# Modulation pieces summed on VectorE and recurrent gates in tiles of whole blocks, in a two-block transformer kernel

## What is computed

```python
mod = (c_act @ w_ada[l] + b_ada[l])[:, None, :]
shift1, scale1, gate1, shift2, scale2, gate2 = jnp.split(mod, 6, axis=-1)
h = _rmsnorm(x, norm1_w[l]) * (1.0 + scale1) + shift1
y = _mixer(h, w_in[l], conv_w[l], a_log[l], ...)
x = x + gate1 * y
...
x = x + gate2 * _moe(h, w_router[l], ...)
...
# second block, for each of two layers and each half of a layer:
shift, scale, gate = ada_modulation(c, ada_w[i, 0], ada_b[i, 0])      # c @ w + b, split in three
h = x * (1.0 + scale) + shift
...
# recurrent_block: 16 blocks of 96 channels
z = h @ w_in
xr, gate = jnp.split(z, 2, axis=-1)
xr = centred_depthwise_conv(xr, conv_w, conv_b)                       # width 4
# rg_lru, for each of two directions:
r = sigmoid(einsum("bsni,nij->bsnj", xb, w_a) + b_a)                  # xb: xr as 16 blocks of 96
i = sigmoid(einsum("bsni,nij->bsnj", xb, w_x) + b_x)
log_a = -LRU_C * r * softplus(-lam)
u = sqrt(-expm1(2.0 * log_a)) * (i * x)                               # then a scan over the tokens
...
y = (forward + backward) * gelu(gate)
return y @ w_out
```

## Time and profile before

| what | us |
|---|---|
| runs: median (lowest to highest) of 3 | 3147.55 (3144.09 to 3152.57) |
| profiled execution, its own time | 3149.12 |
| its span | 3147.5 |
| mean granted TensorE clock | 0.956 |
| TensorE busy | 2889.9 (92%) |
| DVE busy | 1041.6 (33%) |
| ACT busy | 465.0 (15%) |
| POOL busy | 207.1 (7%) |
| transfers | 641.86 MB in 172,530 packets |

### The profile page before, as it was taken

The page is one execution under the profiler, slowest core; times in us unless marked ns, Lnnn a source line. Parts: engine busy times, 40 slices in busy tenths (PEclk is TensorE's granted clock), DMA queues, the critical chain, the costliest instruction groups (busy, mean ns, idle before and its releaser), DMA issues.

```text
span 3147.5 us, 37633 instructions
## 1 busy us (share of the span) xinstructions
PE 2889.9 (92%) x15855; PEld 1424.3 (45%) x15855; DVE 1041.6 (33%) x1367; ACT 465.0 (15%) x915; POOL 207.1 (7%) x308
## 2 busy tenths in 40 slices
PE   6998979699899999998996989999999998999998
PEld 3446565432233333333332465466643333547664
DVE  3304443502111111111114244445443453345544
ACT  1112032100000000000001142000023452200001
POOL 1000011011111101111011100000000010000000
PEclk9999988699999999999997999999998999999999
DMA  8255920599999999999998031212131113212210
GB/s 295 107 214 212 357 62 26 211 342 368 403 370 406 404 401 400 404 404 401 406 387 316 1 115 53 80 54 107 62 103 45 51 40 127 74 54 107 92 68 27
DMA packets 172530, 641.86 MB, mean 204 GB/s; under 512 B 28195, under 2 KB 38011, under 8 KB 131377
## 3 DMA queue, kind: packets, MB, share of 16 engines
q1 hardware_dynamic: 160098, 610.11, 50.4%
q0 software_dynamic: 12208, 29.38, 3.3%
q10 hardware_dynamic: 64, 0.07, 0.0%
HBM read 628.80 MB, written 15.23 MB: 205 GB/s over the span
## 4 chain that ended last, share of the span: by engine, by line
PE 55%; issue 32%; DMA 3%; DVE 3%; POOL 2%; POOLq 2%; ACT 2%; DVEq 1%; SPq 0%; ACTq 0%
PE ps L2357 9%; PE ps L2392 9%; PE ps L2684 4%; PE ps L2428 4%; PE ps L457 3%; PE ps L2927 3%; PE ps L2072 3%; PE ps L2324 2%; PE ps L2343 2%; PE ps L2239 2%; PE ps L1149 2%; POOLq L1592 2%; DMA slots<-in_ada_w_dram 2%; PE ps L356 2%; PE ps L492 1%
## 5 line engine op out<-in xcount | busy, mean ns | idle before, releaser
L1703 PE MATMUL ps<-slots,hT 128*32 128x512 f32 x5120 | 580.8, 599 | 17.4 <-DMA slots<-in_w_up_dram 6.5
L1703 PEld LDWEIGHTS ps<-slots,hT 128*32 128x32 f32 x5120 | 162.6, 110 | 410.8 <-issue 392.9
L2392 PE MATMUL ps<-slots,work 128*128 128x512 f32 x672 | 290.0, 593 | 5.1 <-DVE work L2468 2.8
L1739 PE MATMUL ps<-slots,work 128*32 128x512 f32 x2112 | 253.1, 605 | 29.5 <-DMA slots<-in_w_down_dram 20.8
L1854 DVE TENSOR_SCALAR stage<-ps 128x512 f32<-128x512 f32 (+1 forms) x47 | 32.2, 686 | 581.0 <-PE ps L1705 580.6
L2392 PEld LDWEIGHTS ps<-slots,work 128*128 128x128 f32 x672 | 127.2, 190 | 166.2 <-issue 161.7
L2357 PE MATMUL ps<-hT,slots 128*128 128x256 f32 x768 | 169.2, 380 | 5.1 <-issue 5.1
L1739 PEld LDWEIGHTS ps<-slots,work 128*32 128x32 f32 x2112 | 89.5, 111 | 160.2 <-issue 128.8
L2357 PEld LDWEIGHTS ps<-hT,slots 128*128 128x128 f32 x768 | 145.4, 190 | 29.5 <-issue 9.9
L2684 PE MATMUL ps<-hT,slots 128*128 128x512 f32 x352 | 157.7, 604 | 0.4
L2565 DVE TENSOR_TENSOR work<-work,ps 128x1024 f32<-128x1024 f32 x60 | 71.6, 1218 | 168.5 <-PE ps L2392 168.2
(11 more groups left out here) (571 smaller groups left out, 3467.5 us busy)
## 6 DMA issues: line engine op xcount, KB each, us to landing
slots<-in_w_up_dram SPq DMA_DIRECT2D x128, 2048.0 KB, 19.6
slots<-in_w_down_dram SPq DMA_DIRECT2D x64, 2048.0 KB, 18.9
slots<-in_mlp_w_dram SPq DMA_DIRECT2D x32, 2048.0 KB, 11.7
slots<-in_ada_w_dram SPq DMA_DIRECT2D x24, 1024.0 KB, 7.1
slots<-in_ada_w_dram SPq DMA_DIRECT2D x12, 2048.0 KB, 8.9
slots<-in_w_ada_dram SPq DMA_DIRECT2D x16, 1024.0 KB, 5.8
slots<-in_rnn_w_in_dram SPq DMA_DIRECT2D x8, 1536.0 KB, 7.1
slots<-in_w_in_dram SPq DMA_DIRECT2D x5, 2048.0 KB, 14.4
```

Source lines behind the costliest of these rows:

```text
L1703: ins = pe.matmul(to, x[:, k, unit * UNIT:(unit + 1) * UNIT], upw[s][:, k % 2, col:col + CH], start=k == 0, stop=False)
L1739: ins = pe.matmul(to, actT[:, 4 * q + j, 64 * u + 32 * h:64 * u + 32 * h + 32], downw[sl[h]][:, j, half * CH:(half + 1) * CH], start=k == ...
L2392: ins = pe.matmul(ps[:, bank + t], x[:, k, t * P:(t + 1) * P], w[:, k], start=k == 0, stop=k == HK - 1)
```

## The change

1. N_SIDE is 20, and these pieces are summed on VectorE (`side_dve`): each half times its column of c, added up over the eight halves of a group (40 instructions of 128 x 2048), two behind each convolution from the third on, then 4, 3, 1 and 12 among the scalars' work. TensorE only adds up the 128 partitions (`side_pe`: four matmuls against ones, then the bias), five times. The halves go through slot 2; the window's q weights take slot 5 again, loaded behind half-pieces 6. Twelve pieces are left to the DeltaNet: two ahead of the rounds and one in each of rounds 0 to 9. ACT's `ada_act` calls move accordingly.
2. The scalars' product is turned round: the weights, 8 columns in 32, are stationary, hT moves, in four column groups; ACT copies the bank, and four short matmuls against a table of ones (`absel`), inside the first z block, add up the groups and turn the result.
3. In the routing the counts have a signal of their own ahead of the ranks, and DVE copies `place` behind the table.
4. The recurrent channels are laid out by whole blocks: three blocks of 96 in rows 0 to 95 of a batch's three tiles, the thirds of the fourth in their rows 96 to 127; behind each convolution one copy of 32 x 512 gathers the fourth block (`last3`). A tile's gate is four matmuls of 96 rows in four column groups. The zero fills go, the gate weights take 4 transfers a batch instead of 20, rnn_w_in 6 instead of 1 (384 and 128 bytes a piece), rnn_w_out 4 instead of 1, and `rnn_small` 66 instead of 11.
5. POOL issues `mask_load` ahead of the mixer's small loads and the biases. `moe_sp` ends with one wait on `freed` instead of three.

```diff
-        N_SIDE = 12
+        N_SIDE = 20
+        SIDE_SLOT = 2
 
         def ada_slot(n):
-            return 5 if n < N_SIDE else 4 + (n - N_SIDE) % 2
+            return SIDE_SLOT if n < N_SIDE else 4 + (n - N_SIDE) % 2
...
+        def side_sp(sp, n):
+            load(sp, SIDE_SLOT, side_src(n, 0), ada_slots[:, SIDE_SLOT, 0])
+            if n:
+                sp.wait_ge(S("side_free"), n)
+            sp.dma_start(ada_slots[:, SIDE_SLOT, 1], side_src(n, 1)).then_inc(S("side_in"), 16)
...
+                if n == 6:
+                    load(sp, W_SLOT[4], wview(W_IN[:, 2056:2568]))
...
+                part = ada_slots[:, SIDE_SLOT, kk].rearrange("p (j n) -> p j n", j=4)
+                column = cT[:, 0 if g < 2 else 1, k:k + 1]
+                v.drain()
+                if k == 0:
+                    ins = v.tensor_scalar(side_acc(g), part, column, None, ALU.mult)
+                else:
+                    ins = v.scalar_tensor_tensor(side_acc(g), part, column, side_acc(g), ALU.mult, ALU.add)
+                ins.then_inc((freed[SIDE_SLOT], S("side_free"))[kk], 1)
...
+            pe.wait_ge(S("side_free"), 4 * (g + 1))
+            for j in range(4):
+                pe.matmul(ps[32 * j:32 * j + 32, ada_bank(g)], ones[:, 0:32], side_acc(g)[:, j], start=True, stop=False)
+            ada_bias_pe(pe, g)
...
-        W_SLOT = (4, 5, 0, 1, 2, 3)
+        W_SLOT = (4, 5, 0, 1, 5, 3)
...
+        SIDE_SUMS = {(3, 1): 1, (3, 3): 2, (4, 3): 3, (5, 3): 4}
...
-            pe.wait_ge(S("proj_in"), 80)
-            for u in range(TT):
-                for k in range(KT):
-                    ins = pe.matmul(ps[:, 4, u * 8:(u + 1) * 8], hT[:, k, u * P:(u + 1) * P], wab[:, k], start=k == 0, stop=k == KT - 1)
+            pe.wait_ge(S("proj_in"), 96)
+            for kk in range(2):
+                for j in range(4):
+                    ins = pe.matmul(ps[32 * j:32 * j + 32, 7], abw[:, 2 * j + kk], hT[:, 2 * j + kk, :], start=kk == 0, stop=kk == 1)
             ins.then_inc(S("product_ab"), 1)
...
+                        if (i, t, k) == (3, 0, 4):
+                            pe.wait_ge(S("product_ab"), 2)
+                            for u in range(TT):
+                                ins = pe.matmul(ps[:, 4, u * 8:(u + 1) * 8], abpart[:, u * P:(u + 1) * P], absel, start=True, stop=True)
+                            ins.then_inc(S("product_ab"), 1)
...
+                if j >= 2:
+                    side_dve(v, 2)
+            side_dve(v, 4)
...
+            side_dve(v, 3)
...
+            side_dve(v, 1)
...
+            side_dve(v, 12)
...
+            a.wait_ge(S("product_ab"), 1)
+            a.copy(abpart, ps[:, 7]).then_inc(S("product_ab"), 1)
...
-                pe.matmul(ps[0:E, 2, E:2 * E], ones[:, 0:E], mask[:, u], start=u == 0, stop=u == TT - 1)
+                ins = pe.matmul(ps[0:E, 2, E:2 * E], ones[:, 0:E], mask[:, u], start=u == 0, stop=u == TT - 1)
+            ins.then_inc(S("route_product"), 1)
...
-            v.tensor_copy(place, ps[:, 1, 0:TT * E].rearrange("p (t e) -> p t e", t=TT))
-            v.wait_ge(S("route_product"), TT + 2)
+            v.wait_ge(S("route_product"), TT + 3)
             v.tensor_copy(basecap, ps[:, 3, E:3 * E])
             v.tensor_copy(tab[:, 0:E], ps[0:1, 3, 0:E]).then_inc(S("route_step"), 1)
+            v.tensor_copy(place, ps[:, 1, 0:TT * E].rearrange("p (t e) -> p t e", t=TT))
...
+        def rnn_vector(sp, dst, name, row):
+            a = A[name] if row is None else A[name][0, row:row + 1]
+            whole = a.rearrange("a (b q p) -> p (a b) q", q=4, p=RW)
+            thirds = a.rearrange("a (b q t r) -> r (a b) q t", q=4, t=BB, r=32)
+            for t in range(BB):
+                sp.dma_start(dst[0:RW].rearrange("p (b t) -> p b t", t=BB)[:, :, t], whole[:, :, t]).then_inc(S("rnn_in"), 16)
+                sp.dma_start(dst[RW:P].rearrange("p (b t) -> p b t", t=BB)[:, :, t], thirds[:, :, 3, t]).then_inc(S("rnn_in"), 16)
...
+                for t in range(BB):
+                    own, third = c + RW * t, c + BB * RW + 32 * t
+                    if t == 0:
+                        load(sp, i % 3, wview(W[:, own:own + RW]), slots[:, i % 3, :, 0:RW])
+                    else:
+                        sp.dma_start(slots[:, i % 3, :, t * P:t * P + RW], wview(W[:, own:own + RW])).then_inc(landed[i % 3], 16)
+                    sp.dma_start(slots[:, i % 3, :, t * P + RW:(t + 1) * P], wview(W[:, third:third + 32])).then_inc(landed[i % 3], 16)
...
-                for n, r, nr, c, ncol, p0, at in GATE_PARTS:
-                    src = A[name][0, :, 4 * b + n, r:r + nr, c:c + ncol].rearrange("d i j -> i d j")
-                    sp.dma_start(wg[b % 2][p0:p0 + nr, :, j, at:at + ncol], src).then_inc(S(f"wg_in{b % 2}"), 16)
+                for d in range(2):
+                    src = A[name][0, d, 4 * b:4 * b + 4].rearrange("q i j -> i q j")
+                    sp.dma_start(wg[b % 2][0:RW, d, j].rearrange("p (q n) -> p q n", q=4), src).then_inc(S(f"wg_in{b % 2}"), 16)
...
-                for j in range(2):
-                    for p0, n, at, c0, nc_ in GATE_TURNS[m]:
-                        ins = pe.matmul(ps[c0:c0 + nc_, bank + j], wg[b % 2][p0:p0 + n, d, j, at:at + nc_],
-                                        xr[p0:p0 + n, b * BB + m + (1 if p0 == 0 else -1)], start=False, stop=True)
+                    for c in range(4):
+                        at = m * RW + 32 * c if c < 3 else BB * RW + 32 * m
+                        ins = pe.matmul(ps[32 * c:32 * c + 32, bank + j], wg[b % 2][0:RW, d, j, at:at + 32],
+                                        xr[0:RW, b * BB + m] if c < 3 else last3[b], start=True, stop=True)
...
+                v.drain()
+                v.tensor_copy(last3[n // BB][32 * (n % BB):32 * (n % BB) + 32], y[RW:P]).then_inc(S("bank_free"), 1)
...
-                mixer_loads(g); ada_bias_loads(g); mask_load(g); end()
+                mask_load(g); mixer_loads(g); ada_bias_loads(g); end()
```

175 lines of the change are left out of this document (96 added, 79 removed).

## The result

| | before | changed |
|---|---|---|
| median of the runs of this comparison, us | 3149.35 (4 runs) | 3070.14 (4 runs) |
| ratio, 95% interval | | 0.9754 (0.973 to 0.9779) |
| profiled execution, its own time | 3149.12 | 3068.82 |
| its span | 3147.5 | 3067.2 |

The account below looks back on a forecast made before the run. Bounds: transfers to 43 us, TensorE's sequence to 590, MoE's weight stream, then TensorE nearly gapless in the recurrent stage. Gains 1.5 + 19 + 19 + 3.1 + 38 = 80.6 us from 3149.1 give 3068.5, median 3067, range 3048 to 3095.

Parts of the forecast that it names:

- Head: Before the projections: thirteen small transfers on POOL's queue, said to carry little, move later; 1.5 us gain, between nothing and 3.
- Projections: Up to the DeltaNet stage: pieces moved to VectorE and the turned scalars' product gain 19 us.
- the stall: First z block: TensorE waits 5.6 us at the four short products for VectorE's convolutions and ACT's copy.
- The burst: End of projections: VectorE's last 12 halves, 3.6 us per half, the last done at 221 to 224 us.
- The landing of 4.7 us: Projections: time taken for each 1 MB half's load to land before VectorE sums it, two in flight.
- DeltaNet: Newton rounds from round 10 on, without filler pieces, take 34 us instead of 53.4: 19 us gain, 15 to 22.
- Routing: Counts signalled alone let DVE start earlier, so the table comes sooner: 3.1 us gain, 2 to 4.3.
- Recurrent stage: Gates of 24 tiles save 1.9 us each, less longer waits for ACT and a copy: 38 us gain, 20 to 47.
- The side stream: Rival: loads of halves pace the projections at 9.8 us a pair, gaining 0 to 5 us there; 3083 to 3087 us; chance 0.09.
- The recurrent chain: Rival: DVE and ACT bound the recurrent stage, leaving about 20 us of gain; 3085 us; chance 0.06.
- The four column groups: Rival: recurrent gate groups run one after another, 6.9 us a tile; 3180 us; chance 0.02.
- The small pieces: Rival: small pieces make recurrent weights late, 43 us a batch against some 27 of work; about 10 expected; 3137 us; chance 0.03.

Follow-up runs that it names:

- e1: Kernel before with only POOL's issue order changed (mask load ahead of the small loads): 3141.5 us against 3145.4, ratio 0.9984.
- the second trace: The changed kernel run once more, unaltered, in another job: 3068.6 us, ratio 0.9748 to the kernel before.
- e3: Kernel before with only the recurrent tiles laid out by whole blocks, loads included: 3108.9 us against 3145.4, ratio 0.9879.
- e4: Kernel before with only the routing's signals changed: 3143.7 us against 3145.4, ratio 0.9992.
- e6: Changed kernel with eight halves ahead of VectorE's wait for the sums of squares and seven behind, instead of three and twelve: 3070.2 us, ratio 0.9772.
- e11: Changed kernel with the scalars' product as before, without ACT's copy and the short products: 3065.2 us, ratio 0.9735.
- e5: Changed kernel with the four short products moved from inside the first z block to ahead of the third: 3064.0 us, ratio 0.9746.
- e7: Changed kernel with the edits of e5 and e6 together: 3063.6 us, ratio 0.9755.
- e9: e7 with the halves' loads bringing only 1024 of 2048 columns, so another output: 3081 us, with tokens routed otherwise.

## Why the prediction was right, and where it was not

The forecast, 3067 us, was 3 us from the measured 3070, and most mechanisms held, but that closeness is partly luck: between the two traces the terms of projections and DeltaNet came out 7 and 8 us too high, those of head and recurrent stage 4 us too low each, and 6.4 us came from a stage that had no term.

- **Head, 1.5 us: too small, 5.4 measured** and 5 to 9 by e1. The step that failed is "they carry little": the small transfers were weighed by their bytes. What they cost was throughput of the stream, 157 and 261 GB/s instead of 356 and 422 in two windows, by their 37% of the engines' time in the second and by SP's slower issues; the windows of before could have been read.
- **Projections, 19 us: too large, 12.1 measured** (17.5 less the head's 5.4; 13.8 in the second trace). Against the mean of the four traces with the old projections (204.9, 200.5, 200.2 and 200.3 us from the first projection product to the DeltaNet stage: before, e1, e3, e4) the changed kernel's two (192.7 and 191.1) gain only 9.6. The mis-sized term is the stall: 9.62 us, not 5.6. VectorE's sum was priced right, 2.35 us, and its round is 8.13 us where it waits for nothing (101.71 to 109.84 us), but it also waited for halves between the convolutions, 1.50 us at 122.68 and 0.61 at 132.80; I had let the loads wait only in the last burst. Its last convolution ended 100.9 us behind the first projection product where 97.3 were forecast, and TensorE was at the short products 92.5 us behind it where 93.3 were. Behind it the clock, 0.68 over the 10.5 us that follow: the short products and the 24 records behind them took 14.8 us, where 10.7 (7.1 for 16 records), the short products' 1.2 and my 1.7 make 13.6. Then TensorE waits 0.66 us for the last sum, and the barrier waits for ACT's four issues, 1.1 us that the chain behind the last half left out. The four, 4.0, 1.2, 0.7 and 1.1 us, make up the 6.9 us that are missing. The burst's 3.6 us per half held, but not its place: it ended at 225.7 instead of 221 to 224, and counted from the first projection product at 188.3 us where 178 to 181 were forecast, since VectorE had waited 9.18 us for TensorE before it (in e6, where other halves fill that wait, it ended 182.0 us behind). The landing of 4.7 us (4.9 measured) rested on a wrong reading: the sixteen loads with 5.8 us stand not in the head but at 101 to 186 us, in the projections, and the 7.1 us row mixes eight loads of the projections (5.8 us) with sixteen of the DeltaNet stage (7.3 us). And the base was high: the old product's 11.3 us to the first z product, which I counted as saved, is 9.2 to 9.4 in e1, e3 and e4, though again 11.2 in e11.
- **DeltaNet, 19 us: 11.3 between these two traces,** yet the term is about right. From round 10 on, which it priced, 18.6 us were gained (53.4 to 34.8); rounds 0 to 9 lost 2.3. The rounds together gave 16.3 (116.5 to 100.2; over the traces of before, e1, e3 and e4 the mean is 117.3, over the changed kernel's two 99.4: 18). The 5.0 lost before the first residual looks like scatter: that stretch is 33.3, 38.3, 38.3 and 36.0 us in these four and 33.2 to 39.2 in the others, with TensorE's clock 0.61 over its last 12 us in one trace and 1.00 in the other.
- **Routing, 3.1: 3.3 measured** in every trace with it; in the time of e4 alone it isn't told from nothing.
- **Recurrent stage, 38: 41.9 between the two traces, 39 on the mean.** The gates' 1.9 us per tile held at the higher level, and the growing waits (4.5 and 4.6 us where 3.8 each were taken) nearly. The sum itself had a slip: 46 - 7.6 - 1.2 is 37, and 38 was entered. What I had not priced is the first step at the lower level, 14.8 us of gates that became 6.4: it gives 8.4 us where two tiles were priced at 3.8, and it is there that the traces of before differ.
- **MoE, 0: 6.4 between the two traces,** 1.6 between before and the second.

The rivals. The side stream paced the end of the projections, though at 7.3 us a pair and not at 9.8: the rival's mechanism is real (e5, e7, e9) at three quarters of its price. In the changed kernel itself TensorE waited for the last half only 0.66 us, so the two ended nearly together. The recurrent chain took 9.1 us where 7.6 were forecast, far from the rival's bound. The four column groups run side by side. The small pieces: a batch of six loads, from the window that holds it,

```profile
2388.00:2397.00 9.00, 8.74 (x45) 3.45 (x45) 8.33 (x9) 4.45 (x6) 0.00 (x0) 1.00 0.78 177
```

keeps the 16 engines busy for 0.78 x 9.00 = 7.0 us, where one transfer of 1536-byte pieces did for 0.65 x 7.00 = 4.6 (2412 to 2419 us of the kernel before). That is under my 10 us and far under the 27 from which it decides. By the Trainium skill (DMA: Bandwidth & Descriptors, Specifications) pieces under 512 bytes miss line rate; the trace agrees, 177 GB/s at a share of 0.78 where the 1536-byte pieces made 224 at 0.65. No wait of TensorE for them shows in the stage, so the loads are hidden all the same.

## What to carry to other kernels

Work moved off the critical engine takes its supply with it: price the spacing of the loads (landing plus use, over the places for them) from the first piece on, not only the instruction. A small product turned round did not pay here (e11), since the copy that it needs stood behind VectorE's full program; place such a copy's reader where the copy is done anyway (e5), and look what ends last behind it. And compare more than one trace of before, stage by stage, before a stage's length enters a sum: here three stretches scatter by 2 to 6 us.

## What was not expected of the hardware

- Small transfers of one queue, thirteen issued by 8.5 us, took 37% of the engines' time from 10 to 15 us for 0.07 MB. The whole throughput of 10 to 15 us was 261 to 301 GB/s in the four traces that have them there, against 419 to 428 in the changed kernel's two and e1, and SP's four issues took 5.7 to 6.5 us instead of 2.5 to 2.6.
- Two 1 MB places with a 2.35 us use give one half per 3.6 us; three places 2.7, though a load then lands in 6.7 us instead of 4.9; half the size only 3.0.
- After 7.6 us of waiting (e5) TensorE's next eight records took 1.93 us instead of 1.06. The granted clock had fallen within the wait already: 1.00 over 216.0 to 218.0 us, 0.61 over 218.0 to 221.4, and 0.50, the level of 1.2 GHz, over 221.4 to 223.4.
